# First mixture of experts: TensorE's program as two loops over fixed weight slots, all matmuls on column tiles of 64

## What is computed

```python
logits = x2 @ w_router + b_router
top_vals, top_idx = lax.top_k(logits, 2)
gates = softmax(top_vals)
# for every expert e, on the tokens that chose it:
h = xb @ w_in[e]                              # 1024 -> 2 * 2816
yb = (silu(h[:, :2816]) * h[:, 2816:]) @ w_out[e]   # 2816 -> 1024
y = y.at[token].add(yb * gate)
```

## Time and profile before

| | us |
|---|---|
| median of 3 runs | 1989.19 (1988.69 to 1997.52) |
| profiled execution, its own time | 1990.12 |
| span of its trace | 1988.2 |
| stage of the eight experts, first to last matmul | 536.4 to 1307.9 |
| TensorE busy in the whole span | 1868.9 (94%) |
| mean granted clock of TensorE | 0.984 |
| loads of first-matrix weights | 176 of 1024 KB |
| loads of second-matrix weights | 128 of 704 KB |

### The profile page before, as it was taken

The page is one execution under the profiler, slowest core; times in us unless marked ns, Lnnn a source line. Parts: engine busy times, 40 slices in busy tenths (PEclk is TensorE's granted clock), DMA queues, the critical chain, the costliest instruction groups (busy, mean ns, idle before and its releaser), DMA issues.

```text
span 1988.2 us, 48287 instructions
## 1 busy us (share of the span) xinstructions
PE 1868.9 (94%) x22384; PEld 1494.4 (75%) x22384; DVE 516.1 (26%) x1215; ACT 246.8 (12%) x633; POOL 159.5 (8%) x307
## 2 busy tenths in 40 slices
PE   8999999999999999999999999989989999989775
PEld 7758884666699999998999898977757778753321
DVE  2631000233310101010110101026774433242223
ACT  2310000033110000000000000012222212110000
POOL 0000000100028000000000000036440000000000
PEclk9999999999999999999999999989999999999898
DMA  7224343423399998989898989862301008669996
GB/s 312 99 105 183 145 169 110 167 107 128 144 357 371 347 381 333 374 329 399 311 402 318 389 324 389 325 255 76 123 26 65 34 34 327 268 257 428 427 426 281
DMA packets 72230, 499.31 MB, mean 251 GB/s; under 512 B 8121, under 2 KB 16849, under 8 KB 34513
## 3 DMA queue, kind: packets, MB, share of 16 engines
q1 hardware_dynamic: 61888, 490.12, 62.6%
q10 hardware_dynamic: 10128, 5.97, 1.0%
HBM read 494.99 MB, written 1.05 MB: 249 GB/s over the span
## 4 chain that ended last, share of the span: by engine, by line
PE 86%; DMA 6%; DVE 4%; issue 1%; ACT 1%; ACTq 1%; DVEq 0%; SPq 0%
PE pb L1143 24%; PE pb L1162 12%; PE pb L781 11%; PE pb L790 7%; PE pb L786 4%; PE pb L854 3%; PE pb L1039 3%; DMA ringbuf<-in_e2out 2%; PE pb L1321 2%; PE pb L1298 2%; PE pb L1587 2%; PE pb L1084 2%; DMA arena<-in_e2in 2%; DMA ringbuf<-in_e2in 2%; PE pb L1309 1%; PE pb L1251 1%
## 5 line engine op out<-in xcount | busy, mean ns | idle before, releaser
L1143 PE MATMUL pb<-arena,ringbuf 128*64 128x80 f32 (+1 forms) x9856 | 479.3, 240 | 2.9 <-issue 2.5
L1143 PEld LDWEIGHTS pb<-arena,ringbuf 128*64 128x64 f32 (+1 forms) x9856 | 463.3, 145 | 21.5 <-issue 7.0
L1162 PE MATMUL pb<-arena,ringbuf 128*64 128x80 f32 (+1 forms) x4928 | 232.4, 239 | 7.1 <-issue 6.9
L1162 PEld LDWEIGHTS pb<-arena,ringbuf 128*64 128x64 f32 (+1 forms) x4928 | 228.2, 145 | 10.9 <-issue 8.8
L1649 DVE TENSOR_TENSOR arena<-arena,pb 128x160 f32<-128x160 f32 (+3 forms) x130 | 48.0, 369 | 677.0 <-ACT arena L2616 432.6
L781 PE MATMUL pb<-XT,ringbuf 128*128 128x256 f32 (+2 forms) x1104 | 201.7, 345 | 0.8 <-ACT XT L2417 0.8
L781 PEld LDWEIGHTS pb<-XT,ringbuf 128*128 128x128 f32 (+1 forms) x1104 | 180.4, 192 | 21.9 <-issue 2.1
L2417 ACT ACTIVATE arena<-pb 128x256 f32<-128x256 f32 (+4 forms) x164 | 68.6, 439 | 456.4 <-PE pb L1162 114.0
L790 PE MATMUL pb<-arena 64*64 64x64 f32 (+4 forms) x664 | 106.7, 324 | 5.9 <-DVE Y L1649 3.4
L2616 ACT ACTIVATE arena<-pb 128x160 f32<-128x160 f32 x88 | 26.7, 303 | 580.8 <-PE pb L1143 580.7
L790 PEld LDWEIGHTS pb<-arena 64*64 64x64 f32 (+4 forms) x664 | 52.0, 153 | 56.9 <-issue 29.2
(11 more groups left out here) (391 smaller groups left out, 1842.6 us busy)
## 6 DMA issues: line engine op xcount, KB each, us to landing
ringbuf<-in_ein SPq DMA_DIRECT2D x176, 1024.0 KB, 8.8
ringbuf<-in_eout SPq DMA_DIRECT2D x128, 704.0 KB, 5.9
arena<-in_e2in SPq DMA_DIRECT2D x13, 2048.0 KB, 26.1
ringbuf<-in_e2in SPq DMA_DIRECT2D x12, 2048.0 KB, 34.9
ringbuf<-in_fin SPq DMA_DIRECT2D x11, 2048.0 KB, 8.6
ringbuf<-in_e2out SPq DMA_DIRECT2D x8, 2048.0 KB, 31.0
ringbuf<-in_wo SPq DMA_DIRECT2D x6, 2048.0 KB, 8.5
arena<-in_e2out SPq DMA_DIRECT2D x6, 2048.0 KB, 33.3
```

The costliest lines, as they stand in the source:

```text
L1143: ins = pe.matmul(PB[b][h_, t * C1:(t + 1) * C1], w3[:, k, t * 128 + h_.start:t * 128 + h_.stop], XG[e % 2][:, k, :], start=k == 0, stop=k ...
L1162: ins = pe.matmul(PB[d // 4][h_, (d % 4) * C1:(d % 4 + 1) * C1], w3[:, f, h_], HT[:, f, :], start=f == 0, stop=f == 21)
```

## The change

All of it concerns the first mixture.

- *Slots.* The experts' chunks leave the plan of the ring. The same four slots become four halves for the first matrix (`IN1`, slots 0 and 1: block f lies in halves 2(f mod 2) and 2(f mod 2) + 1) and four for the second (`OUT1`, slots 2 and 3). Each half has a semaphore of its own. Block 0 of an expert counts on separate semaphores (`first_in`), so that blocks 1 to 10 are five equal pairs.
- *Loads.* `load_in` and `load_out` issue one half at a time, each when TensorE has used the half that lay there before (`in_free`, `out_free`). The sizes stay. The first matrix lies in memory so that each half is contiguous. The order is all blocks of the first matrix of an expert, then all of the second. Two blocks of each are loaded ahead of the stage, after all earlier chunks.
- *TensorE.* Per expert: block 0, the turn of the former expert, a device loop (`Fori`) of five passes over blocks (1,2), (3,4) to (9,10), then the scatter, the gather, and a device loop of four passes over output blocks (0,1) to (6,7). Waits inside the loops compare with registers that the loop counts up. Expert 0 writes out its first pair of each loop, expert 7 its first pair of output blocks, with the transposition for the later mixer behind it.
- *Column tiles.* All matmuls are split in two of 64 columns: 128 records in a block, 88 in an output block.
- *Copies.* Output blocks alternate between banks 0 and 1. ScalarE copies the even ones (`even_dims`), VectorE the odd ones (`odd_dims`), 80 columns each.
- *VectorE* adds the scattered rows after its eleventh product, no longer after its third.
- *After the stage* the next chunks wait for the loops' last uses of the slots (`loop_free`). The overflow path reads the first matrix in its new layout.

The diff, cut to its core:

```diff
-        for e in range(NE1):
-            add("ein", dr["ein"][e], [inP.at((1, e, f)) for f in range(11)])
-            add("eout", dr["eout"][e], [dnP.at((1, e, d)) for d in range(8)])
...
+        IN1 = [ringbuf[:, 2048 * k:2048 * k + 2048] for k in range(4)]
+        OUT1 = [slots1[2 + k // 2][:, 1408 * (k % 2):1408 * (k % 2) + 1408] for k in range(4)]
+        def in_free(e, f, x):
+            if e == 0 and f < 2:
+                return cleared[f % 2]
+            return inP.at((1, e, f - 2, x) if f >= 2 else (1, e - 1, 10 if f == 0 else 9, x))
+        def out_free(e, d, x):
+            if e == 0 and d < 2:
+                return cleared[2 + d % 2]
+            return dnP.at((1, e, d - 2, x) if d >= 2 else (1, e - 1, 6 + d, x))
...
+            def up_half(e, f, x):
+                w3 = IN1[in_slot(f, x)].rearrange("p (j n) -> p j n", j=8)
+                for t in (2 * x, 2 * x + 1):
+                    for k in range(8):
+                        for h_ in HALF:
+                            ins = pe.matmul(PB[4 + f % 2][h_, t * C1:(t + 1) * C1], w3[:, k, (t % 2) * 128 + h_.start:(t % 2) * 128 + h_.stop],
+                                            XG[e % 2][:, k, :], start=k == 0, stop=k == 7)
+                return ins
+            def up_pairs(e, first):
+                with pe.register(f"hid{e}") as hid:
+                    pe.reg_mov(hid, 11 * e + 2 * first)
+                    with pe.Fori(16 * (5 * e + first + 1), 16 * (5 * e + 6), 16) as landed:
+                        for f in (1, 2):
+                            pe.wait_ge(hnD.sem, hid)
+                            for x in range(2):
+                                pe.wait_ge(loop_in[in_slot(f, x)], landed)
+                                up_half(e, f, x).then_inc(inP.sem, 1)
+                            pe.reg_add(hid, hid, 1)
+            def down_pairs(e, first):
+                with pe.register(f"read{e}") as read, pe.register(f"even{e}") as even:
+                    pe.reg_mov(read, 4 * e + first)
+                    pe.reg_mov(even, 16 * (4 * e + first + 1) + at_out)
+                    with pe.Fori(16 * (4 * e + first + 1), 16 * (4 * e + 5), 16) as odd:
+                        for d in range(2):
+                            pe.wait_ge((ytD if d else ytA).sem, read)
+                            for x in range(2):
+                                pe.wait_ge(loop_out[out_slot(d, x)], odd if d else even)
+                                down_half(d, x).then_inc(dnP.sem, 1)
+                        pe.reg_add(read, read, 1)
+                        pe.reg_add(even, even, 16)
...
             for e in range(NE1):
                 for q in range(2):
                     pe.wait_ge(*xgD.at((1, e, q)))
-                for f in range(11):
-                    w3 = take("ein")
-                    b = 4 + f % 2
...
-                    if f == 0 and e:
-                        turn(e - 1)
-                    if f == 2 and e:
-                        scatter(1, e - 1, PGT, YS)
+                if e:
+                    pe.wait_ge(*hnD.at((1, e - 1, 10)))
+                for x in range(2):
+                    pe.wait_ge(first_in[x], at_first[x] + 16 * (e + 1))
+                    up_half(e, 0, x).then_inc(*inP.up((1, e, 0, x)))
+                if e:
+                    turn(e - 1)
+                else:
+                    up_pair(e, 0)
+                up_pairs(e, 0 if e else 1)
+                if e:
+                    scatter(1, e - 1, PGT, YS)
                 if e + 1 < NE1:
                     gather(1, e + 1, [ysA.at((1, e - 1)), ysD.at((1, e - 1))] if e else [pgA.at((1, 0)), xgD.at((1, 0, 1))], PS, PG, XG)
...
-                for d in range(8):
-                    w3 = take("eout", 22)
...
+                if e == 0 or e == NE1 - 1:
+                    down_pair(e, 0)
+                if e == NE1 - 1:
+                    s5_turn(dup, [btA.at(0), btA.at(1)], "dup", ctP)
+                down_pairs(e, 1 if e == 0 or e == NE1 - 1 else 0)
...
+            def load_in(e, f):
+                for x in range(2):
+                    k = in_slot(f, x)
+                    sp.wait_ge(*in_free(e, f, x))
+                    sp.dma_start(IN1[k], dr["ein"][e, f, x]).then_inc(loop_in[k] if f else first_in[x], 16)
+            def load_out(e, d):
+                for x in range(2):
+                    k = out_slot(d, x)
+                    sp.wait_ge(*out_free(e, d, x))
+                    sp.dma_start(OUT1[k], dr["eout"][e, d][:, 1408 * x:1408 * x + 1408]).then_inc(loop_out[k], 16)
...
+            for e in range(NE1):
+                for f in range(2 if e == 0 else 0, 11):
+                    load_in(e, f)
+                for d in range(2 if e == 0 else 0, 8):
+                    load_out(e, d)
```

More of the change, by code:

```diff
@@ L111 @@
 NVEC = _a
-PARTS = 2
 class Sig:
@@ L148, with __init__ @@
 class Chunks:
-    def __init__(self, plan, slots, sems, where=None, in_parts=()):
-        self.plan, self.slots, self.sems, self.taken, self.in_parts = plan, slots, sems, 0, in_parts
+    def __init__(self, plan, slots, sems, where=None, pause=None, between=None):
+        self.plan, self.slots, self.sems, self.taken, self.pause = plan, slots, sems, 0, pause
         self.value = []
@@ L157, in __init__ @@
             s = self.where[i]
-            count[s] = count.get(s, 0) + 16 * (src.shape[1] if len(src.shape) == 4 else len(self.parts(i)))
+            if i == pause:
+                count = {k: count[k] + 16 * between[k] for k in count}
+            count[s] = count.get(s, 0) + 16 * (src.shape[1] if len(src.shape) == 4 else 1)
             self.value.append((sems[s], count[s]))
@@ L162, in dst @@
         return self.slots[self.where[i]][:, 0:self.plan[i][2]]
[L164 to L168, removed]
     def before(self, i):
-        return max((k for k in range(i) if self.where[k] == self.where[i]), default=None)
+        first = self.pause if self.pause and i >= self.pause else 0
+        return max((k for k in range(first, i) if self.where[k] == self.where[i]), default=None)
     def take(self, name):
@@ L566, in build @@
         last = [where[n1 - RING + i] for i in range(RING)]
-        base = [0] * 4 + [max(n_ for s_, n_ in ring.value if s_ is s_ring[k]) for k in last] + [0] * 2
+        base = [16 * 5 * NE1] * 4 + [max(n_ for s_, n_ in ring.value if s_ is s_ring[k]) for k in last] + [16 * 4 * NE1] * 2
         ring2 = Halves(plan2, late, s_ring2[0:4] + [s_ring[k] for k in last] + s_ring2[4:], base)
@@ L599, in plan_o1 @@
         def plan_o1(e):
-            return ([(dr["ein"][e, i], SLOT) for i in range(11)],
+            return ([(dr["ein"][e, i].rearrange("x p n -> p x n"), SLOT) for i in range(11)],
                     [(dr["eout"][e, d], DFF) for d in range(8)])
@@ new lines, in down_pairs @@
+            def down_pairs(e, first):
[10 more added lines that the diff above has]
+                        pe.reg_add(even, even, 16)
+                dnP.looped([(1, e, d, x) for d in range(2 * first, 8) for x in range(2)])
@@ L1189, in overflow @@
                             for f in range(s.nf):
-                                if f % 2 == 0:
+                                if f % 2 == 0 and s.nc == 8:
+                                    w, at = s.ring.take(s.kin)
+                                    pe.wait_ge(*at)
+                                    gate3, up3 = [w[:, 2048 * x:2048 * x + 2048].rearrange("p (j n) -> p j n", j=8) for x in range(2)]
+                                elif f % 2 == 0:
                                     w3 = take(s.kin, 8, s.ring)
+                                    gate3, up3 = w3[:, :, 0:256], w3[:, :, 256:512]
                                 b = 4 + f % 4
@@ L2954, in chunk @@
                     sp.wait_ge(*plan[k][3])
-                for cs in ring.parts(i):
-                    sp.dma_start(ring.dst(i)[:, cs], plan[i][1][:, cs]).then_inc(ring.value[i][0], 16)
+                elif i >= nu:
+                    sp.wait_ge(*loop_free[where[i]])
+                sp.dma_start(ring.dst(i), plan[i][1]).then_inc(ring.value[i][0], 16)
                 at[0] += 1
```

123 lines of the change are left out of this document (75 added, 48 removed).

## The result

The changed kernel takes 1971.75 us (median of 4 runs, 1966.17 to 1976.56), the kernel before 1989.91 beside it on the same chip: a ratio of 0.9903, interval 0.9882 to 0.9924. It is faster by 1.0%; the forecast was 2.8%. In the profiled executions the stage of the eight experts went from 771.3 to 749.1 us, first to last matmul start, where 714 was forecast; the whole span shrank by 23.8 us, to 1964.4. So the gain lies in the stage, and of the 57 us forecast there 35 are missing.

A forecast was written before the change was run, and what follows sets the result against it. The prediction took TensorE to bound the kernel, with the DMA close behind and becoming the bound after the change. Stage: 630 + 82.4 + 1.5 = 714 us, 57 less than 771.5; 1990.1 - 57 gave 1934 us, range 1900 to 2002.

The forecast's parts named there:

- TensorE's chain: TensorE's own time in the eight-expert stage without waits for weights: 82.4 us per later expert, 654 in all.
- the DMA becomes the bound: Both expert loops: loads need 4.99 us per first-loop block against TensorE's 4.50, and 3.70 against 3.09 per output block.
- the hole: Between an expert's two loops, over scatter and gather: the DMA idles 5.5 us per expert, waiting to load output block 2.
- code and loop edges: TensorE's stage: fewer code reads, some 30 instead of 124, and about 0.3 us per taken loop branch, hidden by slack.
- rival B: TensorE's loops: code is read again at each of 53 taken branches, about 3 us each, giving 2032 us; chance 0.16.
- a loop's edge: A taken backward branch in TensorE's loops: about 0.3 us each, 16 us on its chain of 654, hidden by slack.
- In the loops there is none.: DMA within both loops: no idle gaps, since next bytes flow 1.0 us after a half is freed, with three halves queued.
- since the queue will be better filled: Loads of the second matrix: reason for taking 390 GB/s, where rows showed 370 and 386.
- the sum: Stage's DMA work plus gaps: 90.0 us per later expert, 630 for seven, plus 82.4 and 1.5, in all 714 us.
- Rival C: Stage's loads: the DMA gets no faster than its slower stretches, 370 GB/s, giving 778 us and 1997 total; chance 0.08.
- I count their end as nothing, since the DMA is the bound: TensorE's standstills for late code, 6.9 us in eight experts before the change: their end was credited with no gain.

The follow-up runs named there:

- e9: Changed kernel with only a quarter of the columns of each expert load loaded, all matmuls kept (output not the reference's): 1860.1 us, ratio 0.935.
- e3: Changed kernel with the next expert's block 0 issued ahead of output block 2, only the order of loads differing: 1955.1 us, ratio 0.983.
- e10: e1's straight code with only a quarter of the columns of each expert load loaded (output not the reference's): 1862.1 us, ratio 0.935.
- e1: Changed kernel with both of TensorE's device loops written out as straight code, all else kept: 2043.5 us, ratio 1.027 to the kernel before.
- e8: e3 with each half of the second matrix contiguous in device memory: 1953.7 us, ratio 0.983 to the kernel before.
- e7: Changed kernel with every second slice of both contractions left out, all loads kept (output not the reference's): 1930.7 us, ratio 0.971.

## Why the prediction was right in sign and wrong in size

**Right: TensorE's chain.** Halves run at 34.4 ns (35.1 forecast). A later expert without waits for weights takes 80.9 us (82.4), the stage 641.5 (654) in e9.

**Right: the DMA becomes the bound.** A block of the steady first loop takes 4.98 us (4.99 forecast), at 422 GB/s.

**Right: the hole.** The DMA stands still for 5.2 us in each of the second to seventh experts (5.5 forecast, with 0.4 for the landing, for which no row stood), over the end of the scatter, the gather and the first half of output block 0, as the fourth window above shows. The order of the queue makes it: e3 reduces it to 0.4.

**Right: code and loop edges; rival B is wrong.** 49 code reads instead of 124 (some 30 forecast), and e9 and e10 agree within 2 us; the 0.3 us taken for a loop's edge was nothing. The Trainium skill, Runtime: NRT & Kernel Launch, section Instruction fetch mechanics, says that a taken branch out of a two-page window stops for a read, and that TensorE's memory holds 128 KiB; the trace agrees with the second for a loop body of 33 KB, and not with the first. It also calls the crossing of a 16 KiB boundary "mostly hidden": here e10 agrees (4 us) and e1 doesn't (114 us).

**The failed step: "In the loops there is none."** The forecast gave a freed half 1.0 us to its next bytes plus 1.7 for them, 2.7 in all, concluded that the halves queued meanwhile keep the DMA full, and so took 390 GB/s for the second matrix, "since the queue will be better filled". The single load that goes out behind the hole shows what it takes (issued at 785.9; KB, us from issue to landing):

```profile
ringbuf<-in_eout SPq DMA_DIRECT2D x1, 704.0 KB, 4.2
```

4.2 us, of which 1.0 passes before its first packet, as forecast; its packets take 3.2, and the landing follows within 0.1. The next load takes 6.1 and those behind them up to 7.2. TensorE uses four halves up in 4 x 1.52 = 6.1 us, so in the second loop it comes back to a slot before the next load has landed there, and by then all four slots wait for loads. (In the first loop four halves last 4 x 2.20 = 8.8 us against a landing of 7.4, and there the step held nearly.) The DMA isn't idle meanwhile (share 0.96), so no gap appears; its packets are slow. One of 5632 bytes takes 0.22 us on average in blocks 0 and 1, which are queued behind the first loop's loads, 0.29 in the first two halves behind the hole and 0.25 over all twelve. These twelve take 26.2 us from the first packet to the last landing, 330 GB/s for their own bytes, where the sum has 12 x 1.85 + 0.4 = 22.6: 3.6 us more per later expert.

What the runs say of the cause: it is not the pause ahead of these loads (26.0 us with the hole closed, e3), nor the layout (26.1, e8), nor a rate of their own or TensorE at work beside them (415 GB/s in blocks 0 and 1, with TensorE busy throughout that window). Where slots come free after half the work, the twelve take 24.0 us (e7), and the stage is 712.4 us, close to the forecast's 714. So 2.2 of the 3.6 us go when the slots are freed sooner. Why the other 1.4 stay, these runs don't show.

The Trainium skill, DMA: Bandwidth & Descriptors, section Anatomy of one DMA, gives about 2.0 us besides the bytes, most of it after the last byte, for the gpsimd path; by that page 704 KB would be 3.7 us, an estimate. The 4.2 us on SyncE's queue are near it in sum, but as the packets are recorded hardly any of it lies behind the last one.

**The same as a rate.** Without its hole an expert moved 34.6 MB in 94.4 - 5.2 = 89.2 us, 388 GB/s, where 23.07 MB at 420 and 11.53 at 390 had made 84.5 us. Over the whole stage an engine is without a packet for 55.8 us, near the 51 of the sum's gaps; the packets' own times are 693.3 where the sum has 663. So 30 of the missing 35 us are slow packets and not gaps. Rival C had named this, but for all loads at 370 GB/s; steady stretches of both matrices move 415 to 426.

**Wrong: "I count their end as nothing, since the DMA is the bound"**, of late code. In the kernel as changed it nearly holds (12.6 us of standstills in the first loop, a part of what it took over the sum). But it hid what the loops are for: without them the change is 2.7% slower than the kernel before (e1).

**The balance.** Six experts at 94.4 - 90.0 = 4.4 us make 26.5 (3.6 of each are the twelve halves behind the hole, the rest mostly the loads from the next expert's block 0 to output block 1), the first is 91.0 against 82.4, 8.6 (its second loop 6.9 of it, measured with the step to the next expert), and the last as forecast: 35 us, the difference of 749 and 714.

**What stays open.** An expert of e3 still takes 92.0 us where its bytes at 420 GB/s are 82.4. Some of the first packets of the slow stretch take 1 us and more, where they take 0.2 to 0.3 in a full queue, with the hole before them (up to 1.3) and without it (up to 1.1, e3); that is seen and not explained. Whether one more slot, in a device loop, would end it was not tried.

## What to carry to other kernels

With fixed slots, compare the engine's time for all slots (6.1 us here) with the whole return of one (the issue, and the transfer behind those queued ahead, 6 to 7 us here), not with its first bytes. Judge an edit against a hole of the DMA by its idle time and its packets' own times together, since a hole that is closed can come back as slower packets, and don't read a DMA share of 0.96 as full speed. Straight code with short instructions and heavy loads beside it may be bound by its own code reads, and there a device loop is worth more than its edges cost.

## What was not expected of the hardware

- TensorE's straight code stalls behind weight traffic: 114 us in a stage of 826 at full loads (e1), 4 us at a quarter of them (e10), with the same 196 code reads.
- A loop body of two blocks, about 33 KB of code, is kept: the stage's reads fell from 141 (e1) to 49, and its passes show no price.
- A single 704 KB load on an idle DMA takes 4.2 us, where its bytes at 420 GB/s are 1.7: 1.0 before the first packet, 3.2 over its packets, under 0.1 behind them.
- A DMA share near 1 doesn't mean full speed: 345 GB/s at 0.96 where four slots come free one by one, 348 at 0.97 without a pause ahead (e3), 378 at 1.00 with slots freed sooner (e7), 415 to 426 in a full queue.
